# A two-layer block on one core: contraction blocks of consecutive features, and projections that start on half of their input

## The reference, cut to what matters

```python
h = rms_norm(x, attn_norm_g)
c_q, c_kv, k_pe, rq, rk, rv, rg = split(h @ w_in)       # latent attention | retention
a_out = mla_group(c_q, c_kv, k_pe, ...)                 # 4 heads, causal, 512 columns
r_out = retention_group(rq, rk, rv, rg, ...)            # 4 heads, 512 columns
x = x + concatenate([a_out, r_out]) @ w_out             # contraction over 1024
hc = rms_norm(x, cross_norm_g); m = rms_norm(mem, mem_norm_g)
x = x + memory_cross_attention(hc, m, ...)              # q = hc @ w_q, kv = m @ w_kv, ... o @ w_o
hm = rms_norm(x, moe_norm_g)
x = x + hierarchical_moe(hm, ...)                       # 32 experts, top 2 of one group of 8
```

## Time and profile before

| | us |
|---|---|
| median of 3 runs | 1047.16 |
| lowest, highest | 1042.11, 1048.00 |
| the profiled execution | 1037.59 |
| its span, first to last instruction | 1035.8 |
| TensorE busy in it | 964.1 |
| VectorE, ScalarE busy | 751.4, 618.9 |

### The profile page before, as it was taken

The page is one execution under the profiler, slowest core; times in us unless marked ns, Lnnn a source line. Parts: engine busy times, 40 slices in busy tenths (PEclk is TensorE's granted clock), DMA queues, the critical chain, the costliest instruction groups (busy, mean ns, idle before and its releaser), DMA issues.

```text
span 1035.8 us, 14477 instructions
## 1 busy us (share of the span) xinstructions
PE 964.1 (93%) x5011; PEld 817.3 (79%) x5011; DVE 751.4 (73%) x1086; ACT 618.9 (60%) x926; POOL 18.4 (2%) x38
## 2 busy tenths in 40 slices
PE   6999989989699999999999699999998999999985
PEld 5888857777578777777778589999996788888864
DVE  4658674546789999998899768788897455555464
ACT  4785753563567777777778655666565444344362
POOL 6000000000000000000000000000000000000000
PEclk9999978999899999999999999999999999999998
DMA  9563422423149989989989636457367456555331
GB/s 319 189 229 134 163 82 82 163 81 123 41 170 350 355 314 359 364 329 345 329 326 368 244 102 203 142 174 232 124 239 233 148 177 202 168 197 186 138 122 41
DMA packets 102119, 214.60 MB, mean 207 GB/s; under 512 B 5412, under 2 KB 59904, under 8 KB 96448
## 3 DMA queue, kind: packets, MB, share of 16 engines
q1 hardware_dynamic: 100432, 211.83, 58.2%
q0 software_dynamic: 1360, 2.20, 0.7%
q10 hardware_dynamic: 288, 0.07, 0.0%
HBM read 213.03 MB, written 1.05 MB: 207 GB/s over the span
## 4 chain that ended last, share of the span: by engine, by line
PE 68%; DVE 12%; DMA 10%; ACT 7%; issue 2%; SPq 0%; DVEq 0%; ACTq 0%
PE bank L1700 15%; PE bank L1702 15%; PE bank L1701 15%; DMA stage<-in_expert_w_down_dram 9%; PE bank L2130 5%; PE bank L2131 5%; PE bank L2132 5%; DVE w_lo L361 3%; DVE w_lo L359 3%; ACT w_hi L350 2%; PE bank L1705 2%; DVE xT_lo L1184 1%; PE bank L1904 1%; PE bank L1920 1%; ACT xT_hi L754 1%
## 5 line engine op out<-in xcount | busy, mean ns | idle before, releaser
L359 DVE TENSOR_TENSOR w_lo<-stage,w_hi 128x1024 fp32r<-128x1024 f32 (+3 forms) x206 | 243.7, 1183 | 102.1 <-ACT w_hi L350 101.4
L350 ACT ACTIVATE w_hi<-stage 128x1024 fp32r<-128x1024 f32 (+3 forms) x206 | 211.9, 1029 | 122.0 <-PE bank L1702 67.9
L361 DVE TENSOR_TENSOR w_lo<-stage,w_hi 128x1024 fp32r<-128x1024 f32 (+3 forms) x206 | 243.4, 1182 | 0.8 <-ACT w_hi L353 0.8
L353 ACT ACTIVATE w_hi<-stage 128x1024 fp32r<-128x1024 f32 (+3 forms) x206 | 210.6, 1022 | 11.5 <-DMA stage<-in_expert_w_up_dram 11.0
L1700 PE MATMUL bank<-w_hi,xT_hi 128*128 128x512 f32 (+1 forms) x448 | 176.8, 395 | 10.1 <-DVE xT_lo L1184 5.4
L1702 PE MATMUL bank<-w_hi,xT_lo 128*128 128x512 f32 (+1 forms) x448 | 174.7, 390 | 0.0
L1701 PE MATMUL bank<-w_lo,xT_hi 128*128 128x512 f32 (+1 forms) x448 | 174.6, 390 | 0.0
L2130 PE MATMUL bank<-xT_hi,w_hi 128*128 128x256 f32 x448 | 127.6, 285 | 2.4 <-DVE xT_lo L1184 2.4
L2131 PE MATMUL bank<-xT_lo,w_hi 128*128 128x256 f32 x448 | 127.6, 285 | 0.0
L2132 PE MATMUL bank<-xT_hi,w_lo 128*128 128x256 f32 x448 | 127.5, 285 | 0.0
L1700 PEld LDWEIGHTS bank<-w_hi,xT_hi 128*128 128x128 f32 x448 | 84.6, 189 | 28.3 <-issue 6.7
(11 more groups left out here) (357 smaller groups left out, 1211.6 us busy)
## 6 DMA issues: line engine op xcount, KB each, us to landing
stage<-in_w_in_dram SPq DMA_DIRECT2D x36, 1024.0 KB, 5.2
stage<-in_expert_w_gate_dram SPq DMA_DIRECT2D x64, 512.0 KB, 4.0
stage<-in_expert_w_up_dram SPq DMA_DIRECT2D x64, 512.0 KB, 5.2
stage<-in_expert_w_down_dram SPq DMA_DIRECT2D x32, 1024.0 KB, 4.9
stage<-in_w_gate_up_dram SPq DMA_DIRECT2D x22, 1024.0 KB, 5.1
stage<-in_w_down_dram SPq DMA_DIRECT2D x11, 1024.0 KB, 4.8
stage<-in_cross_w_kv_dram SPq DMA_DIRECT2D x8, 1024.0 KB, 9.2
stage<-in_w_out_dram SPq DMA_DIRECT2D x8, 1024.0 KB, 4.9
```

Of the source, the lines that this page charges most:

```text
L350: nc.scalar.activation(w_hi[:, s, 0:half], stage[:, s, 0:half], ACT.Copy).then_inc(st.half_ready, 1)
L353: nc.scalar.activation(w_hi[:, s, half:cols], stage[:, s, half:cols], ACT.Copy).then_inc(st.hi_ready, 1)
L359: nc.vector.tensor_tensor(w_lo[:, s, 0:half], stage[:, s, 0:half], w_hi[:, s, 0:half].bitcast(F32), ALU.subtract)
L361: nc.vector.tensor_tensor(w_lo[:, s, half:cols], stage[:, s, half:cols], w_hi[:, s, half:cols].bitcast(F32), ALU.subtract).then_inc(st.lo_ ...
```

## The change

1. **Layout.** `columns`, `w_in2`, `gu2`, the router weights and the gains take block k as the features 128k to 128k+127. `turn` reads 128 consecutive features. The gains are loaded as 8 rows of 128 and turned on PE (two more transposes); the experts keep their layout, and get their own copy of the gain (`gather_g`, 32 bytes per partition, declared behind `norm_g`; all that is declared later moves up by 32 bytes).
2. **Gate and up side by side in `w_hi` and `w_lo`.** ACT and DVE write 4 runs of 256 columns for each half (`beside`), and the matmul reads 512 columns in one run. In the second layer's SwiGLU gate and up come in two transfers.
3. **Output projection.** The retention's half of the contraction (features 512 to 1023) goes first: `turn("cat", pairs 2, 3)` and two units stand between the scores and the transposes of the probabilities.
4. **By contraction halves.** The units of the three projections go half by half (both column halves of one contraction half, then the other). The first four transposed blocks of the next input are made once the first 512 features are final, before the last block (`last=`) of the unit then running; for `crossq`, `catc` and `moe` the parts go to the other half of `xT_hi` (`at_k`), so that they don't overwrite what is being read.
5. **Cross attention by pairs of heads.** Queries are turned, scored and applied pair by pair (`cross_scores`, `turn_probs`, `cross_values`).
6. `products`, ACT's list and DVE's list follow that order.

```diff
 def columns(w, c0, n, h):
-    return w.rearrange("(p k) n -> p k n", k=KD)[:, 4 * h:4 * h + 4, c0:c0 + n], 4 * n
+    return w.rearrange("(k p) n -> p k n", k=KD)[:, 4 * h:4 * h + 4, c0:c0 + n], 4 * n
...
+    gather_g = sb("gather_g", [P, KD])
...
-    for w in ("w_out", "cross_w_q", "cross_w_o"):
-        for c in range(2):
-            before += [columns(a[w][0], 512 * c, 512, h) for h in range(2)]
+    for w, halves_of in (("w_out", (1, 0)), ("cross_w_q", (0, 1)), ("cross_w_o", (0, 1))):
+        for h in halves_of:
+            before += [columns(a[w][0], 512 * c, 512, h) for c in range(2)]
...
+        if ups is not None:
+            nc.scalar.activation(beside(w_hi, s, 0), of_both(s, 0), ACT.Copy).then_inc(st.half_ready, 1)
+            act.wait_ge(st.up_landed[s], ups)
+            nc.scalar.activation(beside(w_hi, s, 1), of_both(s, 1), ACT.Copy).then_inc(st.hi_ready, 1)
+            return
...
-            view = src[:].rearrange("p t (q k) -> p t k q", k=KD)
-            for n in range(4):
+            view = src[:].rearrange("p t (k q) -> p t k q", k=KD)
+            for n in pairs:
...
-        turn("cat", xs, [("cat_scaled", T)])
-        for c in range(2):
-            wide(C_OUT + c, U_OUT + 2 * c, xt="cat")
-        turn("crossq", x, [("x_attn", 2)])
+        turn("cat", xs, [], (0, 1))
+        wide_unit(U_OUT + 2, C_OUT, 0, 512, xT_hi, xT_lo, "cat")
+        wide_unit(U_OUT + 3, C_OUT + 1, 0, 512, xT_hi, xT_lo, "cat",
+                  last=lambda: turn("crossq", x, [("x_attn", 1)], (0, 1)))
+        wide_unit(U_CQ, C_CQ, 0, 512, xT_hi, xT_lo, "crossq",
+                  last=lambda: turn("crossq", x, [("x_attn", 2)], (2, 3)))
...
+        splits_to(U_MOE + 1)
+        add_chunk(0, C_CO, U_CO + 2, "x_cross")
         splits_to(U_MOE + 2)
+        low_parts("moe", MOE_G, (0, 1))
         add_chunk(1, C_CO, U_CO + 3, "x_cross")
-        norm([("x_cross", 2)], "moe", MOE_G)
+        stats(x, xs, [("x_cross", 2)], "moe")
+        low_parts("moe", MOE_G, (2, 3))
...
-        splits_to(U_MOE + 2)
-        norm(x, [("x_cross", 2)], "moe", MOE_G)
+        splits_to(U_MOE + 1)
+        high_parts("moe", MOE_G, (0, 1))
+        splits_to(U_MOE + 2)
+        squares(x, xs, [("x_cross", 2)])
+        high_parts("moe", MOE_G, (2, 3))
```

More of the change, by code:

```diff
@@ L1864, in _ @@
             fills(ins, f"s{n}")
+        turn("cat", xs, [("cat_scaled", T)], (2, 3))
+        for c in range(2):
+            chunk_free(C_OUT + c)
+            wide_unit(U_OUT + c, C_OUT + c, 1, 512, xT_hi, xT_lo, "cat")
         for n in range(3):
@@ L1984, in columns_of @@
                         pe.wait_ge(sem(name + "_xg_lo"), kk + 1)
[L1985 to L1986 removed]
+                    ins = three(bank[6][:, :], xg_hi[:, kk], xg_lo[:, kk], w_hi[:, s, 512 * k:512 * k + 512],
+                                w_lo[:, s, 512 * k:512 * k + 512], start=kk == 0, stop=kk == KD - 1)
                 ins.then_inc(st.unit_done, 1)
```

364 lines of the change are left out of this document (235 added, 129 removed).

## The result

The changed kernel is slower: a median of 1051.32 us over 20 runs (1044.43 to 1056.66) against 1047.11 us over 20 runs of the kernel before (1034.87 to 1052.29). The ratio is 1.0053, its 95% interval 1.0029 to 1.0078, so 3 to 8 us are lost where 4.5 were forecast to be won. The profiled execution took 1052.2 us.

The account below looks back on a forecast made before the run. TensorE (93% busy) was taken as the bound, with DMA engines full as well. Terms -2.2 + 0.1 - 1.5 - 0.8 - 0.4 = -4.8, taken as -4.5, gave 1043 us from 1047.2; range 1036 to 1050.5.

Parts of the forecast that it names:

- Retention half first: Scores to output projection: dense work starts at 154.7 us, values gain 2.8, dense start loses 2.0; 0.9 won so far.
- Borders, by pairs of heads: Query projection to cross output projection: 4.5 us ahead, then 7.5, then 7.4 after PE waits 1.1, 0.5, 0.6; 5.3 left.
- The router's border: End of first layer: first router matmul 4.1 us behind the last dense one; 2.2 of the 5.3 us gain remains.
- The remedy named in passing: At the router: DVE's low split placed behind the router's low parts and the add; ranks at 268.5 instead of 270.5.
- The sum of the middle: First layer up to the expert ranks: -2.2 us, ranks at 270.5 against 272.7.
- Gains on PE: Two transposes and two copies of the gains, the second on ACT's way to x's first norm: +0.1 us.
- Experts: Gate and up matmuls 0.0058 us faster each, 4.8 us in 32 experts if PE sets the pace; -1.5 taken.
- the -0.6: Projections with `mT`: 96 matmuls, each 0.006 us faster; gather and other users of that region another -0.2.
- Passes that write four runs: ACT and DVE writes of four 256-column runs into `w_hi` and `w_lo`: 0 taken, upper bound +0.43 us per pass.
- the rival that had the right sign: "Slower": experts' passes writing runs of 256 cost +0.2 us each and DVE becomes the bound; +5.7, 1053 us; chance 0.08.
- Turns: Transposes' weight loads from `x` take 192 ns, contiguous ones 142; 0.1 us per turn, -0.4 in all.
- The clock: Low clock at the scores lasts 4.0 us into dense work, losing 2.0 us; values take 2.7 us at full clock.

Follow-up runs that it names:

- fill: Changed kernel with its banks from the second layer on moved back by two, plus unread matmuls before the third cross scores and the router; ratio 1.0021 to before.
- own: Changed kernel with later banks moved back, router split earlier, cross-attention steps reordered, second pair's scores in its turned queries' banks; ratio to before 0.9968, again 0.9967.
- border: Changed kernel with ACT's split of the experts' second unit ahead of the first parts of the router's input; ratio to before 0.9990.
- two_products: Changed kernel without the experts' gate and up product of low tokens and high weights; experts take 304.5 us, against 307.3 and 304.6.
- pad: Kernel before with 32 unused bytes per partition declared behind the norm gains; ratio 1.0005.
- own_busy: own with unread matmuls in four further waits of PE: behind router and logits, ahead of gather and SwiGLU; ratio to before 0.9974.

## Why the prediction was wrong

The step that failed is the waits between the pieces of the cross attention ("PE waits 1.1, 0.5 and 0.6"), and with it the clock, to which the sum gave no price behind any wait that the change makes. What the runs showed in its place: a wait of 3.43 us with a fall of 3.4 us behind it, falls behind the router's wait and the SwiGLU's as well, and a SwiGLU term of 3.6 us where the sum has 0.

- *Retention half first: right, where the clock lets it.* Its working has 59.5 us from the last score to the first cross score; the changed kernel's two traces have 59.9, before 67.0, and seven other traces, with the fall near 178 us, 62.0 to 62.4. The first dense matmuls ran at half speed for 3.2 us (157.8 to 161.0; 4.0 taken), the values at full speed.
- *Borders, by pairs of heads: the step that failed most.* "PE waits 1.1, 0.5 and 0.6 between the pieces" was 3.43, 0 and 0.20, and the stretch is 23.8 us where the working had 20.3. The prediction claims to hold each start at its engine, its input and its bank, but doesn't show this chain; the trace has the exponentials behind the root over both pairs, and the third scores behind the exponentials by their bank. Of the 3.5 us, 1.7 are the fall (fill, with the same chain and no fall, has 22.1) and 1.8 the longer wait. own's order, also without a fall, has 20.7. All the shift that the pairs should have brought was lost here.
- *The router's border: right.* 4.1 us of wait forecast, 4.07 measured; last dense matmul to ranks 15.5 against 16.0, with a fall of the clock at 267 that the sum didn't have (fill, without it, has 15.7). The remedy named in passing was worth 4.3 (border), more than the 2.0 worked out.
- *The sum of the middle.* -2.2 forecast, +1.6 to +2.3 measured (123.0 and 123.1 against 121.4 and 120.8), and over +5 in the two other traces with this middle (126.6).
- *Gains on PE.* Sized at +0.1 for their own instructions, which the traces neither confirm nor refute (PE's first turn for x stands at 60.4 to 61.9 us in the three of the old order and at 60.5 to 62.1 in the others). What they did to the table of banks was not looked at: 0.8 us of wait (3.36 against 2.50 to 2.58) and, with the clock behind it, 3.6 us in the SwiGLU. The sum has 0 for that stage, reasoned from its transfers alone.
- *Experts.* The pace fell to 0.2286 us, forecast as 0.228, by the move of 32 bytes and not by the pieces. The row that it was inferred from does not bear it out: `mT` kept its 0.233, so the -0.6 for it was 0, and so was the gather's part of the -0.2 (0.245 us between its matmuls, before and now). The -1.5 was too much: two_products shows that PE's time there is free. Two traces of one kernel differ by 6.8 us in that stretch, so a remainder of about a microsecond can't be excluded.
- *Passes that write four runs: right.* DVE's took 1.22 us in the experts, as before the change, so the rival that had the right sign was there for a wrong reason.
- *Turns.* Weight loads from `x` fell from 192 to 162 ns, and the 16 of the SwiGLU's turn from 2.04 to 1.97 us. So the step costs 30 ns, not the 50 that the comparison with `slot_of` gave. The rule of the Trainium skill ("Advanced Engine Details and Errata", SBUF Cachelines) agrees with the loads; the 0.8 us per turn that it would have made did not come.
- *The clock.* The sum priced one low stretch, at the scores, and nothing behind the waits that the change makes or lengthens. In the changed kernel's first trace each of the three brought a fall of 3.4 us; the falls at 222 and 266 us came back in the second, and the one at the SwiGLU was 6.8 us long there.

Together: +2 in the middle, clock included, and +3.6 at the SwiGLU make +5 to +6, against 5.6 by the measured ratio (0.53% of 1047) and 4.2 between the medians. That it fits so well is luck in part, since the middle alone is 1.6 to over 5 us by where the clock falls. The range ended at 1050.5 and the median is 1051.3: it held one slow case, priced at a bottleneck that is none, and none in which the change's own waits cost the clock.

## What to carry to other kernels

When a step is split into parts, list what each part still waits for as a whole (here one root over all heads, one bank in turn). The split wins nothing until the last of them is split too, and with several chains ending together one must remove all to see any. An entry more in a rotating table moves all later ones: compare the waits far behind the edit as well. And a wait is priced with the clock behind it. Measure a change's stretches from a common event, since two traces of the same kernel differed by 14.6 us, and don't read a rule off one trace: the falls near 178 and 222 us came and went under the same instructions.

## What the runs showed of the hardware

```profile
L384 DVE TENSOR_TENSOR w_lo<-stage,w_hi 128x1024 fp32r<-128x1024 f32 x61 | 74.4, 1219 | 1.5 <-ACT w_hi L371 1.3
```

This group of the changed kernel (300 to 590 us) writes in four runs of 256: 1219 ns, no more than in one run (1218 in the same stretch of before). Moving `xg_hi` and `xg_lo` by 32 bytes took 5 ns of 233 off each matmul of 512 columns (pad), whether the other side was read in one piece or two, and the same move did nothing for `mT`. In the changed kernel's trace the clock was 0.50 for 20.5 us of scores and transposes in which PE was busy for 19.85, and went to 1.00 at 161.0 us, 3.2 us after the first matmul of 512 columns. Falls stand behind waits as short as 1.9 us (own_busy, at 223), and the same wait in own has none.
